# GpSimd's order in a hybrid attention trunk: a weight block's two parts formed in two later steps of its group

## What is computed

```python
h = rmsnorm(x, g_norm[layer]) * (1.0 + scale[:, None, :]) + shift[:, None, :]
z = h @ w_in[layer]
q_sb, k_sb, v_sb, q_fx, k_fx, v_fx, g_path, f_logit = jnp.split(z, split_points, axis=-1)
# stick-breaking, for each block of 128 queries:
log_rem = jnp.where(causal, jax.nn.log_sigmoid(-z), 0.0)
after = lax.cumsum(log_rem, axis=3, reverse=True) - log_rem
a = jnp.where(causal, jnp.exp(jax.nn.log_sigmoid(z) + after), 0.0)
# forgetting:
logits = logits + cum_q[..., :, None] - cum[..., None, :]
p = jax.nn.softmax(jnp.where(causal, logits, -jnp.inf), axis=-1)
# and then
y = jnp.concatenate([rmsnorm(o_sb, ...), rmsnorm(o_fx, ...)], axis=-1) * jax.nn.silu(g_path)
x = x + (1.0 + gate[:, None, :]) * (y @ w_out[layer])
return rmsnorm(x, g_final)
```

## Time and profile before

| | |
|---|---|
| runs, median (range) | 832.02 us (829.75 to 833.76) |
| profiled execution, span | 828.7 us |
| mean granted TensorE clock | 0.973 |
| TensorE, matmul busy | 720.7 us (87%) |
| VectorE / ScalarE / GpSimd busy | 490.9 / 408.4 / 390.7 us |
| low part of a block (L540) | 31 instructions, 83.2 us busy |
| high part of a block (L534) | 31 instructions, 34.5 us busy |

### The profile page before, as it was taken

One profiled execution on the slowest core, in us unless ns is written; L12 is line 12 of the kernel. 1 busy time (PEld: TensorE's weight loads), 2 busy tenths in 40 slices (PEclk: granted clock), 3 DMA queues, 4 the chain that ended last, 5 costly groups with the idle time before them and its releaser, 6 DMA issues.

```text
span 828.7 us, 10998 instructions
## 1 busy us (share of the span) xinstructions
PE 720.7 (87%) x3936; PEld 604.4 (73%) x3936; DVE 490.9 (59%) x993; ACT 408.4 (49%) x846; POOL 390.7 (47%) x325
## 2 busy tenths in 40 slices
PE   0257965989999999999989989998899899999996
PEld 0146754768887887888777878887788788788884
DVE  1486663776564567756634676565447765545565
ACT  4027333576457555554645555555556465623132
POOL 2244422535866563467476644665556465221100
PEclk9988997999999999999989999999999999999998
DMA  6553332104245431133342411244432308894223
GB/s 185 183 200 148 129 100 40 35 22 86 98 102 138 108 103 26 26 91 102 88 136 57 102 26 26 77 128 127 152 94 67 85 25 304 243 311 166 68 90 128
DMA packets 64390, 91.57 MB, mean 111 GB/s; under 512 B 5448, under 2 KB 39880, under 8 KB 63824
## 3 DMA queue, kind: packets, MB, share of 16 engines
q1 hardware_dynamic: 57216, 72.17, 30.4%
q0 software_dynamic: 5376, 14.68, 5.6%
q10 hardware_dynamic: 1744, 4.02, 1.2%
HBM read 67.23 MB, written 23.63 MB: 110 GB/s over the span
## 4 chain that ended last, share of the span: by engine, by line
PE 34%; DMA 21%; POOL 19%; issue 9%; DVE 9%; ACT 6%; SPq 1%; DVEq 0%; POOLq 0%; ACTq 0%
DMA w_raw<-in_w_in 15%; PE psum L1376 10%; POOL w_lo L540 6%; DMA work<-in_w_ada_t 5%; PE psum L1290 4%; PE psum L1291 4%; PE psum L1295 4%; PE psum L1364 4%; DVE work L1037 3%; PE psum L1342 3%; POOL w_hi L534 3%; POOL work L554 2%; POOL work L608 2%; DVE stacks L1005 2%; POOL work L614 2%
## 5 line engine op out<-in xcount | busy, mean ns | idle before, releaser
L1290 PE MATMUL psum<-h_hi,w_hi 128*128 128x512 f32 x496 | 209.6, 423 | 23.9 <-POOL h_lo L591 13.5
L1295 PE MATMUL psum<-h_hi,w_lo 128*128 128x512 f32 x496 | 197.6, 398 | 0.0
L1291 PE MATMUL psum<-h_lo,w_hi 128*128 128x512 f32 x496 | 197.2, 398 | 0.0
L800 ACT ACTIVATE pt_hi<-psum 128x512 fp32r<-128x512 f32 (+1 forms) x192 | 87.5, 490 | 140.5 <-PE psum L1342 137.3
L1097 DVE TENSOR_TENSOR pt_lo<-psum,pt_hi 128x512 fp32r<-128x512 f32 (+1 forms) x192 | 100.6, 551 | 84.4 <-ACT pt_hi L800 83.4
L608 POOL TENSOR_TENSOR work<-work 128x127 f32<-128x127 f32 (+3 forms) x64 | 77.4, 1211 | 152.2 <-DVE work L1037 152.2
L1290 PEld LDWEIGHTS psum<-h_hi,w_hi 128*128 128x128 f32 x496 | 96.0, 193 | 43.6 <-issue 16.2
L1037 DVE TENSOR_TENSOR_SCAN work<-work 128x128 f32<-128x128 f32 (+3 forms) x64 | 104.1, 1627 | 32.5 <-ACT work L768 32.4
L1342 PE MATMUL psum<-ident,work 128*128 128x128 f32 x576 | 88.8, 282 | 29.9 <-POOL work L614 16.0
L1295 PEld LDWEIGHTS psum<-h_hi,w_lo 128*128 128x128 f32 x496 | 95.5, 192 | 22.2
L1291 PEld LDWEIGHTS psum<-h_lo,w_hi 128*128 128x128 f32 x496 | 96.1, 194 | 16.6
(11 more groups left out here) (141 smaller groups left out, 1291.5 us busy)
## 6 DMA issues: line engine op xcount, KB each, us to landing
w_raw<-in_w_in SPq DMA_DIRECT2D x32, 512.0 KB, 9.4
work<-in_w_ada_t SPq DMA_DIRECT2D x24, 512.0 KB, 9.2
work<-in_x SPq DMA_DIRECT2D x16, 512.0 KB, 6.6
w_split_scratch<-work SPq DMA_DIRECT2D x16, 512.0 KB, 3.4
y_split_scratch<-work SPq DMA_DIRECT2D x10, 512.0 KB, 3.7
work<-forget_scratch SPq DMA_DIRECT2D x8, 512.0 KB, 5.1
work<-in_w_out SPq DMA_DIRECT2D x16, 256.0 KB, 5.6
stacks<-y_split_scratch POOLq DMA_DIRECT2D x4, 1024.0 KB, 6.7
```

Source lines behind the costliest of these rows:

```text
L800: nc.scalar.activation(pt_hi[:, a:e, (g % 2) * P:(g % 2 + 1) * P], bank, ACT.Copy).then_inc(s_thi, 1)
L1290: nc.tensor.matmul(bank, hi, h_hi[:, c_, cols], start=(c_ == 0), stop=False)
L1291: last = nc.tensor.matmul(bank, hi, h_lo[:, c_, cols], start=False, stop=(kind == "f" and c_ == DC - 1))
L1295: last = nc.tensor.matmul(bank, lo, h_hi[:, c_, cols], start=False, stop=(c_ == DC - 1))
```

## The change

In every group of four steps GpSimd formed both parts of the weight block in the group's first step (0, 4, 8, 12). Now the high part is formed in the second step (1, 5, 9, 13) and the low part in the third (2, 6, 10, 14), in each case after the step's probabilities and ahead of its job. The first five blocks, which are split before the steps begin, keep both parts together.

```diff
--- before.py
+++ after.py
@@ -525,6 +525,10 @@
                                     base=0, pattern=[[-1, P]], channel_multiplier=1).then_inc(s_mask, 1)
 
             def split_w(b):
+                split_w_hi(b)
+                split_w_lo(b)
+
+            def split_w_hi(b):
 
                 if b >= N_FIRST:
                     before = b - N_FIRST if b < N_FIRST + 2 else b - 2
@@ -532,6 +536,9 @@
                 pool.wait_ge(s_wraw, 16 * (b + 1))
                 hi, lo = w_parts(b)
                 nc.gpsimd.tensor_scalar(hi, w_raw[:], 1.0, 1.0, ALU.mult, ALU.mult).then_inc(s_whi, 1)
+
+            def split_w_lo(b):
+                hi, lo = w_parts(b)
                 pool.wait_ge(s_whi, b + 1)
                 if blocks[b][1] == "f":
                     nc.gpsimd.tensor_tensor(hi[:, :, F_LO:F_LO + 8], w_raw[:, :, 0:8], hi[:, :, 0:8].bitcast(fp32),
@@ -638,8 +645,10 @@
                 if i == 1 and p >= 1:
                     square_pair(p - 1)
                 b = N_FIRST + 4 * p + i // 4 + 1
-                if i % 4 == 0 and b < len(blocks):
-                    split_w(b)
+                if i % 4 == 1 and b < len(blocks):
+                    split_w_hi(b)
+                if i % 4 == 2 and b < len(blocks):
+                    split_w_lo(b)
                 before = (p, i - 1)
                 if before in JOB_AT:
                     do_job(JOB_AT[before])
```

## The result

The changed kernel takes 877.99 us (median of 4 runs, 876.26 to 878.69) against 832.89 us before: a ratio of 1.0525, interval 1.0481 to 1.057. The forecast was 869.2 us with a range of 848 to 883, so the direction and the range held. The narrower band of 855 to 877, which had been given a chance of 0.64, was passed by 1 us, and 9 of 45 us of loss were missed. The profiled execution took 878.69 us, with a span of 876.9 us, 48.2 more than before.

What follows compares the result with a forecast made beforehand. TensorE, busy 720.7 of 828.7 us, was taken to set the end. 10.5 + 10.8 + 3.05 + 4.8 - 0.5 + 6.5 + 2 = 37.2 us made the span 865.9, plus 3.3 for the median: 869.2 us, range 848 to 883.

Steps and rivals of the forecast that it cites:

- Which deadline decides: Third groups of pairs 2, 4, 6: low part, queued behind probabilities, misses the block's opening; 3.5 us each, 10.5 in all.
- The signs named beforehand: TensorE waits on the low part about 20 times, 3.5 us in third groups; VectorE's squares wait falls to about 1.
- First groups: Pairs 2, 4, 6: low part ends 3.9 us later, less 0.3 that step 4 gains; 3 x 3.6 = 10.8 us.
- Second groups: Low part ends about when TensorE opens the block anyway: nothing for pairs 2, 4, 6; 0.4 us for pair 0.
- Fourth groups: High part follows step 15's probabilities: 0.45 us each for pairs 0, 2, 4 and 1.7 for pair 6; 3.05 in all.
- Pair 0: First group's 8.5 us wait changes name, about 0.5 gained; third group loses 4.85; 4.8 us without its fourth group.
- Forgetting pairs: Pairs 1, 3, 5: removed waits and clock, -16.0 - 2.6, against late parts, +6.9 + 2.7 + 8.5; sum -0.5 us.
- The clock: Lower TensorE clock after new waits: five of 3.6 us or more at 1.3, 6.5 us; three of 3.5, 2 us.
- (a): Rival: the backlog is partly given back, so the following group is less late; 854.5 or 849 us; chance 0.17.
- (b): Rival: seven low parts meet a scan at the shared port, 882 us, or squares gain nothing, 880; chance 0.11.
- (c): Rival: the low part is in time at the openings, so only the gain is left; 813 us; chance 0.05.
- (d): Rival: order makes no difference, parts not late before or after, load waits moved instead of removed; 832 us; chance 0.03.

Runs made afterwards that it cites:

- the filler run: Changed kernel plus 12 or 6 matmuls with overwritten results before TensorE's low-part waits at openings of stick-breaking pairs; 869.35 us, 1.0432 to the kernel before.
- the odd pairs alone: Kernel before, with the new order in the forgetting pairs (1, 3, 5) only; 838.39 us, ratio 1.0054.
- the last kernel: Kernel before, with both parts in the second step in forgetting pairs' groups two to four and the job ahead of the weight block there; 832.68 us, 0.9985.

## Why the prediction was right, and where it was off

- **Which deadline decides.** Right. The chain transposes, sigmoids, scan, probabilities, low part was priced at 7.2 us in the third group against 3.7 us until the opening. The opening moved by 3.48 us in pairs 2, 4 and 6; putting the low part ahead of the probabilities removed that wait. The signs named beforehand came: the low part was waited for 26 times (about 20 forecast), the third openings waited 3.23 us (3.5), the wait on the squares fell to 0.91 us (about 1). Pair 2 took 87.3 us, within 86 to 88; pairs 4 and 6, at 90.6 and 91.6, did not, and the difference is the clock's.
- **First groups.** 3.9 us each, as read, with the squares' gain in it. The 0.3 us that step 4 was to give back is hidden in the changed kernel by the clock's loss; in the filler run, at full rate, step 4 of pair 4 takes 5.19 us against 5.48 before.
- **Second groups.** Nothing in the time of the opening, as forecast. But the wait that "should shrink" became one of 2.05 us for the low part, and the forecast did not ask what that does to the clock.
- **Fourth groups.** 0.48 in pairs 0, 2 and 4 (forecast 0.45), 1.5 in pair 6 (1.7).
- **Pair 0.** The 8.5 us wait for the load changed its name to the low part (8.8 us). The weight load left 1.0 us later in this execution (120.33 against 119.33) and the high part began at 137.79 instead of 136.15, so nothing was gained there. The third opening lost 5.2 us against 4.85.
- **Forgetting pairs.** The sum was -0.5 without new clock losses and +0.8 with the one of 1.3 us that was set down for pair 3; measured +2.6. The single terms: first groups 0.8 each (0.9), ends 1.3, 1.3 and 2.0 as net shifts against 2.3 less the wait removed there. The third groups, put at 2.1, 6.1 and 0.3 us, cost 2.9, 5.9 and 1.9 without the clock: the last was too low by 1.6. In the 5.9 us of pair 3 lies the one longer wait for probabilities that was left, 3.8 us (4.5); its clock cost 2.4 us (1.3).
- **The clock: the term that was mis-sized.** 8.5 us were set for it, at 1.3 us for each wait of 3.6 us or more, 2 us for the three of 3.5 and none for shorter ones. Measured over the steps after the waits it is 16.3 us. The failing step is the rule "New waits of 3.6 us and more are like the 3.81 us one", read from single waits, with nothing put for the second openings. A wait of about 2.0 us there cost 1.6 us in pairs 0, 4 and 6 and nothing in pair 2: 4.8 us where the sum had none. The third openings' waits of 3.23 us cost 1.6 in pairs 4 and 6 and nothing in pair 2, 3.2 against 2. The five waits put at 1.3 each cost 8.2 against 6.5. The filler run shows that these losses are the clock's, since they went at the openings where TensorE had work in the wait. This makes 8 of the 11 us by which the span's growth (48.2) exceeded the sum (37.2); the start and the end of the kernel, 1.0 each and not touched by the change, make 2 more, and the last 1.2 us are small differences. The median was missed by less, 8.8 us, because it stands 1.1 us above the span and not 3.3 as assumed; that part is luck.
- **Rivals.** (a), that the backlog is given back, did not happen: openings kept their shift to within 0.1 us. (b) The measured 878 us lies nearer to this rival's 880 to 882 than to the forecast, but neither of its causes occurred: in the steps no low part took over 2.4 us, so no scan held one back, as assumed, and the squares did gain. The holding back went the other way: the 768-wide scan at 315.38, begun 0.92 us after the low part, took 3.03 us, where one of the same width with nothing beside it took 1.76 (at 135.82). The openings kept their shift even so. (c) and (d) fell with the first opening of pair 2.

What stays open: why the same wait costs clock in pairs 4 and 6 and none in pair 2. The runs show only that it does, and that filling the wait ends it. The difference need not lie in the change: step 8 of pair 6 follows the same two waits, 1.33 and 0.71 us, in the kernel before and in the one with the odd pairs alone, and its windows are (before first)

```profile
646.03:651.21 5.18, 5.18 (x33) 1.00 0.63 139
...
654.84:661.62 6.78, 6.78 (x33) 0.75 0.55 131
```

Here too the lower clock costs 1.6 us, after waits that the change left as they were.

## What to carry to other kernels

When an operation is moved down an in-order queue, what counts is the chain that feeds the item it now stands behind, measured from where the consumer itself starts that chain; here two harmless-looking steps put 2.4 us of work behind a loop through four engines. Moving work away from the head of a queue pays where what it waits for is foreign (a load) and not where the consumer is ahead (the even pairs): a smaller move, of both parts by one step in three groups of the odd pairs, gained 1.2%. And a wait on the bounding engine should be priced with the clock that follows it, as a range from nothing to its highest measured cost.

## What the hardware showed that was not expected

- TensorE's granted clock fell after a wait of 2.02 us (0.75 in the next 6.9 us), and in one run after two of 1.33 and 0.71 us, though not after every such wait; 6 matmuls of 512 columns in the wait of 2.02 us, and 12 in those of 3.67 and 3.23 us, kept it at 1.00 in pair 4.
- A 256 KB load issued 2.9 us behind a 512 KB one landed 12.6 us after its issue, in the last kernel, while loads of its kind landed in 6 us in the median of the changed kernel.
- A scan on VectorE that began while GpSimd formed a low part took 3.03 us in place of 1.76; a low part that began just after a scan took 3.42 us in place of 2.34.
